# Linear attention without padded queries: each head's level products on 32 rows of the array, into a bank of its own, in two groups of four levels

## What is computed

```python
x = x + 0.5 * swiglu(rmsnorm(x, ffn1_norm[l]), ...)
h = rmsnorm(x, mix_norm[l])
sq, sk, sv, gq, gk, gv, gg, glr, mq = jnp.split(h @ w_in[l], splits, axis=-1)
y_swa = swa_attention(...)      # 8 heads, window 128
y_gla = gla(gq, gk, gv, gg, glr, ...)   # 4 heads, keys 32 wide, values 64 wide
y_mem = memory_attention(...)   # 4 heads into 256 memory tokens
x = x + jnp.concatenate([y_swa, y_gla, y_mem], axis=-1) @ w_out[l]
x = x + 0.5 * swiglu(rmsnorm(x, ffn2_norm[l]), ...)
```

```python
diff = b[..., :, None, :] - b[..., None, :, :]
decay = jnp.exp(jnp.where(causal[:, :, None], diff, -jnp.inf))
A = jnp.sum(qc[..., :, None, :] * kc[..., None, :, :] * decay, axis=-1)
o_intra = jnp.einsum('bhnij,bhnjd->bhnid', A, vc)
```

## Time and profile before

| | us |
|---|---|
| median of 3 runs | 2083.01 |
| lowest and highest run | 2082.85, 2087.41 |
| span of the profiled execution | 2084.0 |
| busy in it: TensorE, VectorE | 1969.6, 1040.4 |
| busy in it: ScalarE, GpSimd | 474.6, 165.7 |

### The profile page before, as it was taken

How to read it: one execution, slowest core, us unless ns; L and a number is a source line. 1 busy time by engine, 2 the same in 40 slices (tenths; PEclk the granted TensorE clock), 3 DMA queues, 4 the chain that set the end, 5 groups by cost and what they waited for, 6 DMA issues and landing times.

```text
span 2084.0 us, 22231 instructions
## 1 busy us (share of the span) xinstructions
PE 1969.6 (95%) x8562; PEld 1541.7 (74%) x8562; DVE 1040.4 (50%) x1513; ACT 474.6 (23%) x802; POOL 165.7 (8%) x180
## 2 busy tenths in 40 slices
PE   5599999999999999999888889999999999999999
PEld 4488888888888878777544447778888888888887
DVE  4444344433444346258888875363443444344444
ACT  4211111111111124142344442331111111111110
POOL 3000000000000013000343331200000000000000
PEclk9799999999999999999999999999999999999999
DMA  6210111111110200121011011121101111111102
GB/s 195 72 61 31 51 60 40 47 34 60 40 60 21 71 31 1 51 71 31 24 31 30 23 54 60 61 81 41 61 30 50 55 46 40 40 60 40 41 1 81
DMA packets 42432, 103.06 MB, mean 49 GB/s; under 512 B 4995, under 2 KB 17460, under 8 KB 42380
## 3 DMA queue, kind: packets, MB, share of 16 engines
q1 hardware_dynamic: 41440, 100.70, 14.5%
q0 software_dynamic: 704, 1.58, 0.8%
q10 hardware_dynamic: 236, 0.06, 0.0%
HBM read 90.39 MB, written 5.77 MB: 46 GB/s over the span
## 4 chain that ended last, share of the span: by engine, by line
PE 84%; DVE 7%; ACT 3%; issue 2%; DMA 2%; POOL 1%; DVEq 0%; ACTq 0%; POOLq 0%
PE ps L41 27%; PE ps L42 27%; PE ps L43 27%; DMA bias_dram<-bias_row 2%; DVE A_T L1090 2%; PE ps L893 1%; ACT Pg L1016 1%; DVE hT_lo L490 1%; DVE gq_pad L983 1%; PE ps L623 1%; DVE Pg L1076 1%; POOL rstd L517 1%; DVE xT L351 1%; PE ps L878 0%; ACT glu L1026 0%
## 5 line engine op out<-in xcount | busy, mean ns | idle before, releaser
L314 DVE TENSOR_TENSOR ps<-ps,rstd 128x512 f32<-128x512 f32 x88 | 61.5, 699 | 585.1 <-PE ps L43 585.0
L351 DVE SCALAR_TENSOR_TENSOR xT<-ps,xT 128x512 f32<-128x512 f32 x352 | 239.0, 688 | 136.4 <-PE ps L43 136.4
L41 PE MATMUL ps<-hT_hi,hi_b 128*128 128x512 f32 x704 | 278.2, 395 | 23.8 <-DVE glu L320 23.8
L41 PE MATMUL ps<-hT_hi,hi_a 128*128 128x512 f32 x704 | 280.3, 398 | 10.2 <-DVE lo_a L266 8.5
L42 PE MATMUL ps<-hT_lo,hi_a 128*128 128x512 f32 x704 | 278.8, 396 | 0.0
L43 PE MATMUL ps<-hT_hi,lo_a 128*128 128x512 f32 x704 | 278.5, 396 | 0.0
L42 PE MATMUL ps<-hT_lo,hi_b 128*128 128x512 f32 x704 | 278.0, 395 | 0.0
L43 PE MATMUL ps<-hT_hi,lo_b 128*128 128x512 f32 x704 | 277.8, 395 | 0.0
L41 PE MATMUL ps<-act_hi,hi_d 128*128 128x512 f32 x704 | 275.2, 391 | 2.6 <-DVE act_lo L323 1.7
L42 PE MATMUL ps<-act_lo,hi_d 128*128 128x512 f32 x704 | 274.2, 390 | 0.0
L43 PE MATMUL ps<-act_hi,lo_d 128*128 128x512 f32 x704 | 273.9, 389 | 0.0
(11 more groups left out here) (193 smaller groups left out, 2345.3 us busy)
## 6 DMA issues: line engine op xcount, KB each, us to landing
raw_d<-in_w_down SPq DMA_DIRECT2D x44, 512.0 KB, 4.2
raw_a<-in_w_gate SPq DMA_DIRECT2D x22, 512.0 KB, 3.3
raw_a<-in_w_up SPq DMA_DIRECT2D x22, 512.0 KB, 3.3
raw_b<-in_w_gate SPq DMA_DIRECT2D x22, 512.0 KB, 3.3
raw_b<-in_w_up SPq DMA_DIRECT2D x22, 512.0 KB, 4.5
p_raw<-in_w_proj SPq DMA_DIRECT2D x15, 512.0 KB, 3.3
xT<-in_x SPq DMA_DIRECT2D x4, 1024.0 KB, 10.0
p_raw<-in_w_out SPq DMA_DIRECT2D x8, 512.0 KB, 3.3
```

Source lines behind the costliest of these rows:

```text
L41: nc.tensor.matmul(out, w_hi, x_hi, start=first, stop=False)
L314: nc.vector.tensor_tensor(ps[:, BANK_GATE + h, :], ps[:, BANK_GATE + h, :], rstd[:, cols], ALU.mult).then_inc(gate_scaled, 1)
L351: nc.vector.scalar_tensor_tensor(out=dst, in0=ps[:, BANK_DOWN + g % 4, :], scalar=0.5, in1=dst, op0=ALU.mult, op1=ALU.add).then_inc(down_a ...
```

## The change

The pads go, with their zeros, their semaphores and GpSimd's share. VectorE writes the query side of all levels and heads in one product, gq_lv, 128x1024 (gla_queries), placed behind y_lo(0). GpSimd then writes the key side as before (gla_keys). TensorE multiplies for each level and head the 32 rows of that head alone: 32 matmuls of 128x128 in place of 8 of 128x512. Head h has bank 4 + h, and level l the columns of l % 4 in it. The products come in two groups of four levels (levels_part): the first where all eight stood, the second behind turn(0), after the fourth take; each group reports once, at its end. A take now reads one quarter of each of the four banks. The transpose of k_hat waits for the eighth take.

```diff
-                for l in range(LEVELS):
-                    if l >= 4:
-                        wait(pe, level_taken, LEVELS * n + l - 3)
-                    nc.tensor.matmul(ps[:, 4 + l % 4, :], g_lv[:, l, :], gq_pad[l // 4][:, l % 4, :, :],
-                                     start=True, stop=True).then_inc(level_ready, 1)
+                levels_part(0)
+
+            def levels_part(part):
+
+                if part:
+                    wait(pe, level_taken, LEVELS * n + 4)
+                for l in range(4 * part, 4 * part + 4):
+                    for h in range(4):
+                        r = slice(h * GLA_DK, (h + 1) * GLA_DK)
+                        mm = nc.tensor.matmul(ps[:, 4 + h, (l % 4) * P:(l % 4 + 1) * P], g_lv[r, l, :], gq_lv[r, l, :],
+                                              start=True, stop=True)
+                mm.then_inc(level_ready, 4)
...
             turn(0)
+            levels_part(1)
             wait(pe, gla_factor, LF * n + LF - 1)
-            wait(pe, level_taken, LEVELS * n + 7)
+            wait(pe, level_taken, LEVELS * n + 8)
...
-        def gla_pads(dve, n, part):
+        def gla_queries(dve, n):
             wait(dve, gla_exp, 3 * n + 1)
-            for h in (range(2) if part else range(4)):
-                pad_levels(nc.vector, n, part, h, gla_factor)
+            nc.vector.tensor_tensor(gq_lv[:], g_lv[:], gqk[:, 0, blk(n)].unsqueeze(1).to_broadcast([P, LEVELS, P]),
+                                    ALU.mult).then_inc(gla_factor, 1)
...
-                                          ps[:, 4 + l % 4, :].rearrange("p (h q) -> p h q", h=4)
+                                          ps[:, 4:8, (l % 4) * P:(l % 4 + 1) * P]
...
             y_lo(slice(0, 4), 2, 0)
             if not last:
-                gla_pads(dve, n + 1, 1)
+                gla_queries(dve, n + 1)
```

More of the change, by code:

```diff
@@ L60, in build @@
         xT = sb("xT", [P, KT, T])
-        pads = lambda i: phase((f"pad_skip{i}", [P, 4, T], F32), (f"gq_pad{i}", [P, 4, 4, P], F32))[1]
-        gq_pad = [pads(0)]
+        gq_lv = phase(("lv_skip", [P, 4, T], F32), ("gq_lv", [P, LEVELS, P], F32))[1]
         hT_hi = sb("hT_hi", [P, KT, T], F32R)
-        gq_pad.append(pads(1))
         hT_lo = sb("hT_lo", [P, KT, T], F32R)
@@ L163, in build @@
          turned, pt_ready, pv_done, y_hi_ready, y_lo_ready, level_ready, level_taken, gla_diff, gla_exp,
-         gla_factor, pads_ready, k_hat_turned, k_hat_copied, kv_ready, state_ready, o_ready, o_copied) = [sem(n) for n in (
+         gla_factor, factor_ready, k_hat_turned, k_hat_copied, kv_ready, state_ready, o_ready, o_copied) = [sem(n) for n in (
             "staged_q staged_k staged_mq staged_v staged_gv scores_ready biased shift_ready probs_ready denom scaled "
             "turned pt_ready pv_done y_hi_ready y_lo_ready level_ready level_taken gla_diff gla_exp "
-            "gla_factor pads_ready k_hat_turned k_hat_copied kv_ready state_ready o_ready o_copied").split()]
+            "gla_factor factor_ready k_hat_turned k_hat_copied kv_ready state_ready o_ready o_copied").split()]
         const_landed = sem("const_landed")
-        const_set, pads_set = sem("const_set"), sem("pads_set")
+        const_set = sem("const_set")
         x_landed = [sem(f"x_landed{i}") for i in range(4)]
@@ L868, in levels @@
             def levels():
-                wait(pe, gla_factor, LF * n + DVE_PADS)
-                wait(pe, pads_ready, 3 * n + 3)
+                wait(pe, gla_factor, LF * n + 1)
+                wait(pe, factor_ready, n + 1)
                 wait(pe, pt_ready, 3 * n)
@@ L974, in gla_diffs @@
                                            op1=ALU.min).then_inc(gla_diff, 1)
[L977 to L984, removed]
-        def gla_pads(dve, n, part):
+        LF = 3
+        def gla_queries(dve, n):
             wait(dve, gla_exp, 3 * n + 1)
-            for h in (range(2) if part else range(4)):
-                pad_levels(nc.vector, n, part, h, gla_factor)
+            nc.vector.tensor_tensor(gq_lv[:], g_lv[:], gqk[:, 0, blk(n)].unsqueeze(1).to_broadcast([P, LEVELS, P]),
+                                    ALU.mult).then_inc(gla_factor, 1)
         def gla_edge_factors(dve, n):
@@ L996, in gla_edge_factors, with gla_keys @@
             nc.vector.tensor_tensor(q_hat[:], decay[:], q, ALU.mult).then_inc(gla_factor, 1)
[L998 to L1005, removed]
+        def gla_keys(pool, n):
+            wait(pool, gla_factor, LF * n + 1)
             nc.gpsimd.tensor_tensor(g_lv[:], g_lv[:], gqk[:, 1, blk(n)].unsqueeze(1).to_broadcast([P, LEVELS, P]),
-                                    ALU.mult).then_inc(pads_ready, 1)
+                                    ALU.mult).then_inc(factor_ready, 1)
         def mix_scalar(act, n, first, last):
@@ L1112, in mix_vector @@
             if first:
-                dve.wait_ge(pads_set, 2)
-                gla_pads(dve, 0, 0)
-                gla_pads(dve, 0, 1)
+                gla_queries(dve, 0)
                 gla_edge_factors(dve, 0)
@@ L1131, in mix_vector @@
                 gla_diffs(dve, n + 1)
-                gla_pads(dve, n + 1, 0)
             else:
@@ L1187, in mix_pool @@
         def mix_pool(pool, n, first, last):
-            wait(pool, pads_ready, 3 * n + 3)
             def scale(u):
@@ L1200, in mix_pool @@
             if not last:
-                wait(pool, scaled, 12 * n + 12)
-                gla_pads_pool(pool, n + 1)
+                gla_keys(pool, n + 1)
         def mix_start_pool(pool):
@@ L1210, in mix_start_pool @@
             pool.wait_ge(proj_ready, NG)
-            for t in gq_pad:
-                nc.gpsimd.memset(t[:], 0.0).then_inc(pads_set, 1)
             for t in (A_T[:], Pg1[:, :, 0:P]):
@@ L1402, in _ @@
             mix_start_pool(pool)
-            gla_pads_pool(pool, 0)
+            gla_keys(pool, 0)
             each_block(pool, lambda n, first, last: mix_pool(pool, n, first, last))
```

## The result

| | median us | runs | lowest to highest |
|---|---|---|---|
| before | 2083.62 | 4 | 2082.85 to 2087.41 |
| after | 2096.45 | 4 | 2095.99 to 2098.01 |

The ratio is 1.0059, with a 95% interval of 1.0045 to 1.0073: the change makes the kernel 12.8 us slower. Forecast was 2078.7. The time lies inside the range of 2067 to 2098, but on the other side of no change. The profiled execution has a span of 2094.7 us, 10.7 above that of before.

What follows compares the result with a forecast made beforehand. VectorE was taken to bound each mixing block, the TensorE/ScalarE chain being 3.2 us early. Full-clock terms, -16.8 - 6.0 + 9.6 + 0.9 = -12.3, plus 8.0 for the clock gave -4.3: 2078.7 us, range 2067 to 2098.

Steps and rivals of the forecast that it cites:

- 1: Queries on VectorE, per block: six padded writes become one product of 1.22 us, freeing 5.0 us of work.
- 2: TensorE/ScalarE chain behind the takes is late next, k_hat moved by 0.87; gain 2.4 us per block, seven times 16.8.
- 3: Fifth take waits for the second group, 1.14 us on four strips: +1.2 us per block, eight times 9.6.
- 4: First block: without clearing and pads the first take starts 5.4 us earlier, the takes' end 6.0 in all.
- 5: Last block: no queries follow, so nothing is given back, and the later k_hat transpose adds 0.9 us.
- 6: TensorE's clock: one half-clock stretch per block at the critical chain, 1.0 us each, +8.0 in total.
- full-clock sum: Block period if the clock stays full: 27.7 - 2.4 + 1.2 = 26.5 us.
- A: Rival: TensorE's clock holds, or ScalarE hides its cost; 2070.7 us, chance 15%.
- B: Rival: between takes 4 and 5 the strips do not run together on TensorE; 2098 to 2105 us, chance 17%.
- C: Rival, half gain: strips overlap two by two or half clock doubles the second group; 2086 to 2088 us, 14%.
- D: Rival: VectorE's 5.0 us is not freed, the one product being slowed by GpSimd; near 2088 us, chance 2%.

Runs made afterwards that it cites:

- e9: Kernel before with only the query side changed to one VectorE product, TensorE's level products kept, output not the layer's; 2058.06 us, ratio 0.9874.
- e1: Kernel after plus products nobody reads in TensorE's idle stretches: 12 ahead of turn(0), 4 behind it, 12 behind the second group; 2078.30 us, ratio 0.9969.
- e8: e4 plus 12 useless products ahead of turn(0); 2049.28 us, ratio 0.9838 to the kernel before.
- e6: Kernel after with the loops of a group exchanged, head outside and level inside, so four products in a row use the same 32 rows; 2125.37 us, ratio 1.0195.
- e10: Kernel before with level products cut from 512 to 128 columns, still on all 128 rows, three heads left out; 2089.97 us, ratio 1.0023.
- e4: Kernel after with turn(1) in banks 0 and 1, done with values(0) ahead of k_hat, ScalarE copying in matching order; 2070.34 us, ratio 0.9929.

## Why the forecast was right and wrong

**1 held.** The query product took 1.22 us, and VectorE's busy time in a block fell from 23.65 to 18.8, by 4.9 of the 5.0 forecast.

**2 held.** The chain of TensorE and ScalarE was next. e9 shows the reserve of 3.2 us as read, e1 the remaining gain with the chain moved by a take: period 26.7 with the second group's wait, against 26.5.

**3 held at full clock.** 32 records on four strips took 1.17 us (forecast 1.14), and the wait of the fifth take at full clock is 1.38 in e8. The trace of before had no such product; the two-column form L931/L932 was the right row to price it by. That four row strips would do as two column halves do was an assumption, and it came out; with the other loop order (e6, 2.82) it would not have.

**4 and 5 held.** The first take came 5.7 us earlier (forecast 5.4), the end of the first takes 4.2 instead of 4.8, the difference being the doubled second group (0.9) less the 0.3 by which the first take came earlier than forecast. For the last block, e1 has 14.5 us from the last take to the first output matmul against 13.7 before, the 0.9 of part 5.

**6 is the step that failed, by its size.** The direction of the mechanism was right: the clock does go to half in each block behind the thin stretch. The price was 1.0 us per block with an upper end of 1.7 (and 1.1 more for the second group), taken from one stretch of 3.41 us. It is 3.2 us (29.9 less e1's 26.7). The stretch is 13.7 us long and covers turn(0), the second group, k_hat, turn(1) and values(0). All of them but turn(0) are on the path, so nothing of it hides:

| on the path | at full clock (e1) | after | difference |
|---|---|---|---|
| second group | 1.17 | 2.09 | +0.9 |
| k_hat transpose | 0.3 | 0.44 | +0.1 |
| turn(1) | 1.06 | 1.91 | +0.85 |
| values(0) | 1.93 | 3.25 | +1.3 |

The sum is 3.2, so 2.2 per block more than forecast. Seven times that is 15.4, and seven times the 0.2 by which e1's period exceeds the full-clock sum is 1.4: together 16.8, to be compared with the 16.7 by which the seven periods missed (15.3 against -1.4). The first block adds 0.6 and the last 0.5. That is 17.8, the whole way from -4.3 to the 13.5 measured. The step's assumptions failed one by one: that one short stretch would do, though the prediction itself listed three idle stretches close to each other; that half of a slower chain would hide behind ScalarE's copy; and that a second group at half clock was a separate rival of 14% and not the same event. A longer stretch stood in the rows: the first block showed 6.82 us of half clock, around an idle time of 8.29. I priced by the shorter one because the idle times were shorter. Even the row that I took was no firm price: in the execution of after the same place kept full clock. Every block after has 2.81 us, then 0.52, then 3.65 without matmuls, with 2 us of products between, and this was enough for twice the longer stretch.

The Trainium skill (TensorE: Matmul & The Clock Gate, section on oscillation in real kernels) describes a kernel in which each tile's few products are followed by a longer wait, so that the clock is lost again in every tile. The trace agrees in the recurrence: there is a stretch at 0.50 in each of the eight blocks. The waits here are shorter than that kernel's, 2.81 us at most ahead of the fall. It is the periodic form that I should have priced, with all of the critical chain inside.

**Rivals.** A (the clock holds) fell as a forecast, but e1 is its kernel: 2078.3 against its 2070.7. B did not occur in the change, only in e6. C was half right: the second group was doubled, and the half gain lost, together with the long stretch, so that even C's 2088 was too low. D fell.

**What stays open.** No run separates how much idle time, at which spacing, makes the stretch 6.8 or 13.7 us long. e10 shows that strips are not needed for the drop; whether they prolong it is not shown. Why some executions have more half clock than others, as in e1, is not explained. Whether the strip or the bank holds the products of e6 apart, and what e9 would do with e4's order, is not shown. Real work in place of e8's fillers was not tried.

## What to carry to other kernels

Where an engine that runs beside the bound is relieved, look at what it does next: if it is TensorE, and its idle time falls just ahead of work on the critical chain, price that chain at half clock in full, all of it, every period, unless the trace excludes it. The remedies are order (put its remaining work where it would idle, as in e4) and, cheaply, products that nobody reads (e1, e8); test the parts of a change one by one, since here one of them alone was worth -26 us. Products on row strips, each with a bank of its own, should take the strips in turn, strip innermost (1.17 us against 2.82).

## What the hardware showed that I had not expected

- Half clock lasted 13.67 us although TensorE was busy for 8.82 of them; in e10 it lasted 6.80 with 6.36 busy. The clock does not come back as soon as there is work.
- Twelve useless products per block ahead of turn(0) made e4 21 us faster (2070.3 to 2049.3), and 28 per block made the kernel after 18 us faster.
- Four row strips side by side kept the 0.11 us pace each: 32 records in 1.17 us, against 2.82 with the same strip and bank four times in a row.
